# Residuals and layer norms of a two-block kernel: residual added by VectorE from PSUM, squares summed on 32-column tiles, another order of the tail

## The chip, the cores and the metric

One core of one Trainium2 chip runs the whole program. The metric is device time in microseconds (us), the median of several runs; the profile is one further execution, taken by the hardware profiler. Engines: PE is TensorE (PEld its weight loads), DVE is VectorE, ACT is ScalarE, POOL is GpSimd, SP is SyncE. A trailing q (DVEq) is an engine's sequencer.

## The reference, cut to what matters

All is float32. The first block (two layers, 512 latent tokens and 256 context tokens of 1024 channels) feeds a second block; the change touches the end of each mixing part and each feed-forward part of the first block:

```python
x = layer_norm(ALPHA * x + ml[2] * (m @ w_out + b_out), ln1_g, ln1_b)
h = modulate(x, ml[3], ml[4])                  # h * (1 + scale) + shift
x = layer_norm(ALPHA * x + ml[5] * ((silu(dwconv(h @ w_up_a)) * (h @ w_up_u)) @ w_down), ln2_g, ln2_b)
# layer_norm: mean and variance over the 1024 channels of each token, eps 1e-5
```

ALPHA is the square root of 2. Layer 0 does this for latent and context tokens (width W = 768), each stream with its own modulation; layer 1 for the latent tokens alone (W = 512).

## The kernel before

Activations lie channel-major: X is 8 chunks of 128 channels by TOK = 768 tokens. A linear layer is run in units: a unit makes 128 output channels of all W tokens in one PSUM tile. To keep float32 precision, weights and activations are each split in a high and a low part (fp32r), and a unit is three thirds of matmuls, high x high, low weights x high, high weights x low (`unit`, L516). There are four PSUM tiles of 1024 columns; units alternate between two of them (tb and tb + 1), and a semaphore `tile_free` for each tile is raised by whoever empties it. The first two units of a linear layer whose input has just been made run as a pair (`first_pair`, L484), chunk by chunk as high and low parts come in (semaphores h2_hi, h2_lo, ...).

Weights stream through a ring of four slots: SP loads a unit into w_raw, ACT rounds it to w_hi (L1089, `refill`, after the unit that used the slot), and POOL subtracts for w_lo (L447). Each engine runs one instruction list written out in order; semaphores with counted values (`on`, `at_least`) tie them together. The table STAGES only counts how often each stage takes each PSUM tile.

The stages around the change, for each of the two layers: `out` (8 units, tb 0) and norm `ln1`; then `up0`, `down0`, `up1`, `down1`, `up2`, `down2` (the feed-forward channels in parts of 8, 8 and 6 chunks; a unit of down2 has 6 chunks instead of 8; tb 2 for all down stages) and norm `ln2`. After ln1 the modulated input of up0 is made (`modulated`, `modulated_hi`), after ln2 of layer 0 that of layer 1, after ln2 of layer 1 the kernel writes x for the second block. So there are four norm sites: ln1 and ln2, in layer 0 and in layer 1.

How a site works before the change. When unit j is done, ACT moves it from PSUM to SBUF, scaled by the gate (`scaled_residual_unit`, L1172), then refills the weight slot; DVE adds it to X with the factor alpha (L1777 at a norm, L1764 in down0 and down1). The norm's statistics are made while the last units run: a sum over the first four chunks gives a pivot, which PE makes by a matmul with a matrix of ones behind unit 4 (`channel_sum`, L523), and DVE subtracts twice that from each chunk (`pivoted`, L1782); ACT squares each chunk (`layer_norm_square`, L1130) into four buffers, and PE sums squares 0 to 3 behind unit 5, 4 and 5 behind unit 6, and 6, the second half of the mean, and 7 behind unit 7, each with ones of 128x128. Then ACT makes the squared mean and the negated mean (L1136, L1137), DVE the variance (`variance`, L1817), ACT the inverse root as Ln and Exp (L1139, L1141), and DVE adds the negated mean to all chunks (`recentered`, L1809: six before it waits for the root, the last two inside the loop that follows). DVE and ACT then make the modulated input two chunks at a time (L1747, ACT L1116, L1754). At ln2 of layer 0, DVE scales X (L1721) before it raises the last two counts of h_lo (in code behind L1958) that PE waits for; at ln2 of layer 1, DVE scales and shifts each chunk (L1721, L2127).

## Time and profile before

| | |
|---|---|
| median of 3 runs | 3555.5 us (3552.7 to 3559.64) |
| the profiled execution's own time | 3559.22 us |
| its span, first to last instruction | 3557.4 us |
| mean granted TensorE clock over the span | 0.964 of full speed |
| busy: PE / PEld / DVE / ACT / POOL | 93% / 73% / 55% / 35% / 24% |

The busy shares are averages over many stages with different limits. What a site is worth is read from its own stretch: the time from the end of unit 5 to the end of unit 7, and from there to where the next units run unhindered.

### The profile page before, as it was taken

To read this page: it belongs to the slowest core of one execution; us is meant where nothing else is said; L and a number is where in the kernel's file an instruction comes from. 1 tells how busy PE (TensorE), PEld (TensorE's weight loads), DVE (VectorE), ACT (ScalarE), POOL (GpSimd) and SP (SyncE) were. 2 spreads that over 40 slices of the span, in tenths; PEclk is the share of its full clock that TensorE was granted. 3 is DMA by queue.
4 is the path that set the end of the run, shared out by engine and by line. 5 is a ranking of instruction groups with operands and counts; after the bars stand their busy time and mean duration, and the time that the engine had idled before them with its cause. 6 is when DMAs were issued, how large, how long until landed. Compare 5 with 4: busy or idle time off the path is not lost.

```text
span 3557.4 us, 44002 instructions
## 1 busy us (share of the span) xinstructions
PE 3306.4 (93%) x15976; PEld 2583.6 (73%) x15976; DVE 1971.0 (55%) x2633; ACT 1244.2 (35%) x1742; POOL 847.6 (24%) x336
## 2 busy tenths in 40 slices
PE   6999899998889999978999998899997999999997
PEld 4778677787778888856776777588875775677665
DVE  4678987624375252547789854565464534253333
ACT  2112253233233222233225334442235344443533
POOL 1002102222222232320020233244442221332211
PEclk9999899999999999989999999999998989998999
DMA  6541101112111211114510123132231120221111
GB/s 259 172 166 48 36 1 48 48 48 94 43 48 54 71 62 63 60 65 166 198 60 13 60 65 113 54 101 95 95 98 54 53 65 26 75 83 54 54 37 58
DMA packets 72957, 272.08 MB, mean 76 GB/s; under 512 B 8545, under 2 KB 9057, under 8 KB 71905
## 3 DMA queue, kind: packets, MB, share of 16 engines
q1 hardware_dynamic: 71360, 256.04, 21.7%
q10 hardware_dynamic: 1440, 13.89, 1.0%
q8 instruction: 107, 1.75, 0.2%
q14 instruction: 50, 0.40, 0.0%
HBM read 264.66 MB, written 5.24 MB: 76 GB/s over the span
## 4 chain that ended last, share of the span: by engine, by line
PE 81%; DVE 9%; ACT 3%; DVEq 2%; issue 2%; DMA 1%; ACTq 1%; SPq 0%
PE ps L516 47%; PE ps L758 11%; PE ps L484 4%; PE ps L523 3%; PE ps L586 2%; PE ps L707 2%; DVE x L1903 2%; DVE arena L1895 2%; PE ps L894 1%; PE ps L574 1%; PE ps L871 1%; PE ps L607 1%; PE ps L729 1%; PE ps L992 1%; PE ps L973 1%
## 5 line engine op out<-in xcount | busy, mean ns | idle before, releaser
L447 POOL TENSOR_TENSOR w_lo<-w_raw,w_hi 128x1024 fp32r<-128x1024 f32 x332 | 847.4, 2555 | 2670.5 <-ACT w_hi L1089 2670.3
L516 PE MATMUL ps<-act_hi,w_hi 128*128 128x512 f32 x2656 | 565.0, 362 | 7.8 <-DVE arena L2064 2.0
L516 PE MATMUL ps<-act_lo,w_hi 128*128 128x512 f32 x2656 | 545.9, 355 | 0.0
L516 PE MATMUL ps<-act_hi,w_lo 128*128 128x512 f32 x2656 | 545.8, 355 | 0.0
L516 PEld LDWEIGHTS ps<-act_hi,w_hi 128*128 128x128 f32 x2656 | 436.9, 189 | 126.3 <-issue 50.8
L1089 ACT ACTIVATE w_hi<-w_raw 128x1024 fp32r<-128x1024 f32 x380 | 399.8, 1054 | 316.9 <-PE ps L516 91.0
L516 PEld LDWEIGHTS ps<-act_hi,w_lo 128*128 128x128 f32 x2656 | 436.3, 188 | 74.0
L516 PEld LDWEIGHTS ps<-act_lo,w_hi 128*128 128x128 f32 x2656 | 436.3, 188 | 73.5
L1903 DVE SCALAR_TENSOR_TENSOR x<-arena,vec,x 128x512 f32<-128x512 f32 x336 | 234.9, 727 | 0.2 <-issue 0.2
L1895 DVE SCALAR_TENSOR_TENSOR arena<-arena,vec 128x783 f32<-128x783 f32 (+1 forms) x240 | 230.2, 959 | 0.0
L2096 DVE SCALAR_TENSOR_TENSOR arena<-arena,vec 128x769 f32<-128x769 f32 (+1 forms) x88 | 159.1, 1808 | 15.3 <-issue 15.3
L1154 ACT ACTIVATE arena<-ps,vec 128x768 f32<-128x768 f32 (+3 forms) x64 | 50.9, 795 | 293.5 <-PE ps L516 197.0
L758 PE MATMUL ps<-act_hi,w_hi 128*128 128x512 f32 x432 | 138.5, 459 | 12.0 <-ACT vec L1124 6.2
L1764 DVE SCALAR_TENSOR_TENSOR x<-x,arena 128x768 f32 (+1 forms) x32 | 32.5, 1016 | 185.7 <-ACT arena L1172 185.7
L1172 ACT ACTIVATE arena<-ps,mod 128x512 f32<-128x512 f32 x72 | 41.7, 614 | 240.7 <-PE ps L516 182.7
L758 PEld LDWEIGHTS ps<-act_hi,w_hi 128*128 128x128 f32 x432 | 88.2, 210 | 47.3 <-issue 29.6
L1686 DVE TENSOR_TENSOR ffn_lo<-arena,ffn_hi 128x768 f32 (+1 forms) x44 | 118.2, 2687 | 7.1 <-issue 1.3
L1777 DVE SCALAR_TENSOR_TENSOR x<-x,arena 128x768 f32<-128x768 f32 (+1 forms) x32 | 34.6, 1082 | 153.5 <-ACT arena L1172 153.5
L707 PE MATMUL ps<-arena 128*128 128x256 f32 (+1 forms) x288 | 103.8, 481 | 15.8 <-ACT tmp L1197 15.8
L758 PE MATMUL ps<-act_lo,w_hi 128*128 128x512 f32 x432 | 111.5, 391 | 5.6 <-DVE act_lo L2161 5.6
L758 PE MATMUL ps<-act_hi,w_lo 128*128 128x512 f32 x432 | 114.8, 400 | 0.0
L1378 ACT ACTIVATE arena<-ps 128x512 f32<-128x512 f32 x66 | 32.4, 526 | 211.2 <-PE ps L516 208.3
(311 smaller groups left out, 4794.7 us busy)
## 6 DMA issues: line engine op xcount, KB each, us to landing
w_raw<-in_weights SPq DMA_DIRECT2D x380, 512.0 KB, 3.5
arena<-in_ada_w SPq DMA_DIRECT2D x75, 512.0 KB, 4.4
tmp<-in_ada_w SPq DMA_DIRECT2D x21, 512.0 KB, 5.1
x<-in_x SPq DMA_DIRECT2D x2, 1536.0 KB, 20.2
x<-in_x ACTq DMA_DIRECT2D x1, 3072.0 KB, 10.1
x_mid<-x ACTq DMA_DIRECT2D x1, 3072.0 KB, 9.7
x<-x_mid ACTq DMA_DIRECT2D x1, 3072.0 KB, 10.2
arena<-in_pool_w ACTq DMA_DIRECT2D x2, 1024.0 KB, 4.8
```

The costliest lines, as they stand in the source:

```text
L447: nc.gpsimd.tensor_tensor(WL[:, w], raw, WH[:, w].bitcast(f32), ALU.subtract).then_inc(units_split, 1)
L484: last = nc.tensor.matmul(ps(tb + s, a, b), w[:, s * UNIT + k * P:s * UNIT + (k + 1) * P], act[:, k * TOK + a:k * TOK + b], start=(n == 0 ...
L516: last = nc.tensor.matmul(ps(t, a, b), w[:, s * UNIT + k * P:s * UNIT + (k + 1) * P], act[:, k * TOK + a:k * TOK + b], start=(n == 0 and k ...
L523: last = nc.tensor.matmul(ps(s, a, b), ONES[:, :], src[:, a:b], start=start, stop=stop)
L586: last = nc.tensor.matmul(ps(3, (m % 2) * 512, (m % 2) * 512 + 2 * P), values(m, k), AR[:, a:a + 2 * P], start=(k == 0), stop=(k == nk - 1))
L707: last = nc.tensor.matmul(ps(it % 2, a, b), AR[:, q:q + P], AR[:, k + a:k + b], start=True, stop=True)
L758: return nc.tensor.matmul(out, w0[:, k0:k0 + P], act[:, k * n:k * n + SEQ], start=start, stop=stop)
L1089: nc.scalar.activation(WH[:, s * UNIT:(s + 1) * UNIT], RAW[:, (s % 2) * UNIT:(s % 2 + 1) * UNIT], ACT.Copy).then_inc(hi_done, 1)
L1686: return V.tensor_tensor(lo, src, hi.bitcast(f32), ALU.subtract)
L1895: t = V.scalar_tensor_tensor(acc, src, w, acc, ALU.mult, ALU.add)
L1903: t = V.scalar_tensor_tensor(acc, src, w, acc, ALU.mult, ALU.add)
L2096: t = V.scalar_tensor_tensor(cv, src, w, cv, ALU.mult, ALU.add)
```

## The change

1. The residual is added by DVE straight from PSUM: one scalar_tensor_tensor for each token stream, PSUM times gate plus X (`residual`). ACT no longer copies these units out; in out, down0, down1 and down2 it only refills weight slots. The factor alpha and the gated bias of ln1's residual are put on X beforehand (a tensor_scalar for each chunk and stream, while `out` begins); the factor for ln2 is folded into the scale and bias with which ACT writes ln1's output.
2. Squares 0 to 6 are summed by matmuls with a 128x32 matrix (first column ones, the others zeros), each chunk into its own 32 rows of the pivot's PSUM tile: 0 to 3 behind unit 6, 4 to 6 inside unit 7, ahead of its last third, followed by the first part of the second mean. ACT copies the result to SBUF, and behind unit 7 one `channel_sum` adds it, one adds chunk 7 to the mean, and one adds square 7.
3. ACT asks for the table set natural_log_exp_and_others as the stage `out` or `down2` begins.
4. The pivot is subtracted from chunks 5 to 7 before their residual is added. The negated mean is made before the squared mean. DVE recenters chunk 0 before the variance, 1 and 2 between variance and root, and 3 to 7 inside the loop that follows.

```diff
+            def unit(s, t, sp_, kt, hi, lo, within=None):
                 for n, (w, act) in enumerate(((WH, hi), (WL, hi), (WH, lo))):
+                    if within and n == 2:
+                        within()
...
+                def squares(cs):
+                    pe.wait_ge(*at_least(l, nm + "_sq", cs[-1] + 1))
+                    for a, b in sp_:
+                        for c in cs:
+                            j, src = 32 * (c % 4), LN_SQ[c % 4]
+                            last = nc.tensor.matmul(PS[j:j + 32, pivot * 1024 + a:pivot * 1024 + b], FIRST[:, :], AR[:, src + a:src + b],
+                                                    start=(c < 4), stop=(c > 2))
+                    last.then_inc(on(l, nm + "_sq_used"), len(cs))
+                def within():
+                    squares((4, 5, 6))
+                    pe.wait_ge(tile_free[tb], taken(l, nm, tb, 0))
+                    pe.wait_ge(*at_least(l, nm + "_summed", 2))
+                    channel_sum(tb, AR[:, SUM:SUM + TOK], sp_, True, False)
...
-                    for c in {5: (0, 1, 2, 3), 6: (4, 5), 7: (6,)}.get(j, ()):
-                        squares(c)
...
+                    if j == 6:
+                        pe.wait_ge(tile_free[pivot], taken(l, nm, pivot, 1))
+                        squares((0, 1, 2, 3))
                     if j == 7:
+                        pe.wait_ge(tile_free[sq], taken(l, nm, sq, 0))
+                        pe.wait_ge(*at_least(l, nm + "_part", 1))
+                        channel_sum(sq, AR[:, LN_SQ[0]:LN_SQ[0] + TOK], sp_, True, False)
                         pe.wait_ge(*at_least(l, nm + "_centered", CH))
                         channel_sum(tb, X[:, (CH - 1) * TOK:CH * TOK], sp_, False, True).then_inc(on(l, nm + "_mean"), 1)
-                        squares(7)
+                        pe.wait_ge(*at_least(l, nm + "_sq", CH))
+                        channel_sum(sq, AR[:, LN_SQ[3]:LN_SQ[3] + TOK], sp_, False, True).then_inc(on(l, nm + "_sq_used"), 1)
...
+            def refilled_norm(l, nm, st, tb):
+                W, pivot = width(l), 2 - tb
+                nc.scalar.preload_act_table_set("natural_log_exp_and_others")
+                for j in range(CH):
+                    act.wait_ge(units_used, unit_done(l, st, j // SLOTS, j % SLOTS))
+                    refill(l, st, j // SLOTS, j % SLOTS)
+                    for c in {4: (0, 1, 2, 3), 6: (4, 5, 6), 7: (7,)}.get(j, ()):
+                        layer_norm_square(l, nm, c, W)
+                    if j == 6:
+                        act.wait_ge(*at_least(l, nm + "_sq_used", 7))
+                        nc.scalar.activation(AR[:, LN_SQ[0]:LN_SQ[0] + W], ps(pivot, 0, W), ACT.Copy).then_inc(on(l, nm + "_part"), 1)
+                        act.drain().then_inc(tile_free[pivot], 1)
...
+            def residual(l, st, gate, tb, j):
+                t = tb + j % 2
+                dve.wait_ge(units_used, unit_done(l, st, j // SLOTS, j % SLOTS))
+                for m, (a, b) in enumerate(spans(l)):
+                    x = X[:, j * TOK + a:j * TOK + b]
+                    last = V.scalar_tensor_tensor(x, ps(t, a, b), at(MOD, mod(l, gate, j, m), 1), x, ALU.mult, ALU.add)
+                return last
...
+                residual(l, st, gate, tb, 4).then_inc(tile_free[tb], 1)
+                dve.drain()
                 dve.wait_ge(*at_least(l, nm + "_mean", 1))
                 for c in range(5):
+                    pivoted(c).then_inc(on(l, nm + "_centered"), 1)
+                for c in (5, 6, 7):
                     pivoted(c)
+                dve.drain().then_inc(tile_free[pivot], 1)
                 for j in (5, 6):
-                    residual(j)
-                    pivoted(j)
-                    dve.drain()
+                    residual(l, st, gate, tb, j).then_inc(on(l, nm + "_centered"), 1)
+                    dve.drain().then_inc(tile_free[tb + j % 2], 1)
                     V.tensor_tensor(sums, x_(4) if j == 5 else sums, x_(j), ALU.add)
...
+                recentered(l, nm, tb, 0)
                 variance(l, nm, tb, dst)
-                for c in range(6):
+                for c in (1, 2):
                     recentered(l, nm, tb, c)
-                dve.wait_ge(*at_least(l, nm + "_root", 3))
+                dve.wait_ge(*at_least(l, nm + "_root", 4))
+            def recentered_pair(l, nm, tb, i):
+                for c in {1: (3,), 2: (4, 5), 3: (6, 7)}.get(i, ()):
+                    recentered(l, nm, tb, c)
...
+                for c in range(CH):
+                    for m, (a, b) in enumerate(spans(l)):
+                        x = X[:, c * TOK + a:c * TOK + b]
+                        V.tensor_scalar(x, x, ALPHA, at(GB, (l * CH + c) * 2 + m, 1), ALU.mult, ALU.add)
...
                         scale_chunk(l, "ln2", "ln2_g", c, W)
-                        if c < 2:
-                            recentered(l, "ln2", 2, c + 6)
+                        if c + 3 < CH:
+                            recentered(l, "ln2", 2, c + 3)
```

## Rows read from the trace of the kernel before

**Rows 1.** The page, part 4: the chain that ended last, by engine.
```profile
PE 81%; DVE 9%; ACT 3%; DVEq 2%; issue 2%; DMA 1%; ACTq 1%; SPq 0%
```

**Rows 2.** Windows of PE: stretch us, length, busy (instructions), granted clock, DMA share, GB/s.
```profile
941.06:975.72 34.66, 28.36 (x120) 0.90 0.11 31
975.72:996.08 20.36, 7.12 (x17) 0.76 0.08 26
1547.22:1577.25 30.03, 24.09 (x96) 0.89 0.06 18
2249.96:2274.92 24.96, 20.00 (x60) 0.86 0.17 61
2651.24:2670.06 18.82, 14.04 (x48) 1.00 0.25 84
1635.00:1645.00 10.00, 10.00 (x45) 1.00 0.63 211
```

**Rows 3.** The chain in order of time, 888 to 1016 us: start, us, what.
```profile
931.22 1.29 PE ps L523 x4
...
967.18 8.48 PE ps L516 x48
```

**Rows 4.** Timeline of PE, 940 to 1016 us: start, us, operation [idle before <-releaser].
```profile
944.19 7.09 PE L523 MATMUL ps<-arena,ones 128*128 128x512 f32 x16 [3.20 <-ACT arena L1130]
...
1011.35 0.97 PE L484 MATMUL ps<-act_hi,w_hi 128*128 128x512 f32 x4 [0.33 <-ACT act_hi L1116]
```

**Rows 5.** Timeline of ACT, 890 to 1016 us.
```profile
904.18 1.23 ACT L1172 ACTIVATE arena<-ps,gate_bias,mod 128x512 f32<-128x512 f32 x2 [13.99 <-issue]
...
985.33 0.81 ACT L1137 ACTIVATE arena<-ps 128x768 f32<-128x768 f32 x1
...
988.43 1.28 ACT L1141 ACT_TABLE_LOAD   x1
...
1015.47 0.87 ACT L1378 ACTIVATE arena<-ps 128x512 f32<-128x512 f32 x2 [1.81 <-PE ps L484]
```

**Rows 6.** Timeline of DVE, 900 to 1015 us.
```profile
905.52 0.96 DVE L1777 SCALAR_TENSOR_TENSOR x<-x,arena 128x768 f32<-128x768 f32 x1 [8.69 <-ACT arena L1172]
...
978.11 0.96 DVE L1782 SCALAR_TENSOR_TENSOR x<-ps,x 128x768 f32<-128x768 f32 x1
...
987.16 6.17 DVE L1809 TENSOR_TENSOR x<-x,arena 128x768 f32<-128x768 f32 x7 [0.21 <-issue]
993.43 2.20 DVE L1747 SCALAR_TENSOR_TENSOR tmp<-x,ln_mod_gain,arena 128x512 f32<-128x512 f32 x4
```

**Rows 7.** Timeline of POOL, 895 to 1020 us.
```profile
978.15 2.35 POOL L447 TENSOR_TENSOR w_lo<-w_raw,w_hi 128x1024 fp32r<-128x1024 f32 x1 [13.69 <-ACT w_hi L1089]
```

**Rows 8.** Timeline of DVE, 2255 to 2370 us (layer 1).
```profile
2265.80 2.42 DVE L1797 TENSOR_TENSOR arena<-arena,x 128x512 f32<-128x512 f32 x1
...
2286.42 1.42 DVE L1747 SCALAR_TENSOR_TENSOR tmp<-x,ln_mod_gain,arena 128x512 f32<-128x512 f32 x2
```

**Rows 9.** Timeline of PE, 1530 to 1660 us.
```profile
1622.82 1.22 PE L484 MATMUL ps<-act_lo,w_hi 128*128 128x512 f32 x2 [4.29 <-DVEq L1958]
...
1633.24 1.07 PE L607 MATMUL ps<-arena,gla_w 128*32 128x512 f32 x8
1634.24 2.12 PE L516 MATMUL ps<-act_hi,w_hi 128*128 128x512 f32 x8
```

**Rows 10.** Timeline of DVE, 2615 to 2735 us.
```profile
2678.76 3.70 DVE L1809 TENSOR_TENSOR x<-x,arena 128x512 f32<-128x512 f32 x6 [0.21 <-issue]
2682.56 0.75 DVE L1721 SCALAR_TENSOR_TENSOR x<-x,vec,arena 128x512 f32<-128x512 f32 x1
```

**Rows 11.** Timeline of ACT, layer 1: 2301 us, then 2713 us.
```profile
2301.82 0.60 ACT L1378 ACTIVATE arena<-ps 128x512 f32<-128x512 f32 x1 [1.13 <-PE ps L484]
...
2713.30 1.28 ACT L1124 ACT_TABLE_LOAD   x1
```

**Rows 12.** Timeline of DVE, 60 to 110 us: two-operand tensor_scalar, 512 and 256 columns.
```profile
69.45 0.75 DVE L1901 TENSOR_SCALAR x<-arena,vec 128x512 f32<-128x512 f32 x2
```

More of the change, by code:

```diff
@@ L165, in two_blocks @@
         MASK = sb("gla_masks", 2 * P, i32)
-        ARENA_N = 20318
+        ARENA_N = 20280
         with nc.sbuf_tensor("arena", [P, ARENA_N], f32) as AR:
@@ L470, in single @@
                     start(i, s)
-                    unit(s, tb + s % 2, sp_, kt, hi, lo).then_inc(units_used, 1)
+                    unit(s, tb + s % 2, sp_, kt, hi, lo, within if within and i * SLOTS + s == CH - 1 else None).then_inc(units_used, 1)
                     if behind:
@@ L748, in block1 @@
                     linear(l, f"down{p}", 2, sp_, n, GH, GL, ready=(("g_split", first), ("g_split", first)), tb=2,
-                           behind=layer_norm(l, "ln2", sp_, 2) if p == 2 else None)
+                           **(layer_norm(l, "ln2", sp_, 2) if p == 2 else {}))
             one = ((0, SEQ),)
@@ L1164, in evacuate @@
                         evacuate_unit(l, st, i, s, dst(i, s, W), func, bias)
-            def scaled_residual_unit(l, st, gate, bias, dst, done, first, tb, i, s):
-                act.wait_ge(units_used, unit_done(l, st, i, s))
-                act.wait_ge(*at_least(l, done, i * SLOTS + (first + s + 1)))
-                act.sem_inc(paced[0], 1)
-                for j, (a, b) in enumerate(spans(l)):
-                    last = nc.scalar.activation(AR[:, dst + s * TOK + a:dst + s * TOK + b], ps(tb + s % 2, a, b), ACT.Identity,
-                                                bias=at(GB, i * 8 + (l * CH * 2 + 2 * s + j), 1) if bias else 0.0,
-                                                scale=at(MOD, i * 8 + mod(l, gate, s, j), 1))
-                last.then_inc(tile_free[tb + s % 2], 1)
-                refill(l, st, i, s)
@@ L1178, in scaled_residual, with refilled @@
-            def scaled_residual(l, st, gate, bias, dst, done, first, tb, nm=None):
-                if nm:
-                    for j in range(CH):
-                        scaled_residual_unit(l, st, gate, bias, dst, done, first, tb, j // SLOTS, j % SLOTS)
-                        for c in {5: (0, 1, 2, 3), 6: (4, 5), 7: (6, 7)}.get(j, ()):
-                            layer_norm_square(l, nm, c, width(l))
-                else:
-                    with act.Fori(0, 2) as i:
-                        for s in range(SLOTS):
-                            scaled_residual_unit(l, st, gate, bias, dst, done, first, tb, i, s)
+            def refilled(l, st):
+                with act.Fori(0, 2) as i:
+                    for s in range(SLOTS):
+                        act.wait_ge(units_used, unit_done(l, st, i, s))
+                        refill(l, st, i, s)
@@ L1386, in block1 @@
                     if p == 0:
-                        layer_norm_out(l, "ln1", "ln1_b", W)
-                    scaled_residual(l, f"down{p}", 5, False, FT, "res2", p * CH, 2, "ln2" if p == 2 else None)
+                        layer_norm_out(l, "ln1", "ln1_b", W, ALPHA)
+                    if p < 2:
+                        refilled(l, f"down{p}")
+                    else:
+                        refilled_norm(l, "ln2", "down2", 2)
                 layer_norm_root(l, "ln2", 2, LN_R, W)
@@ L1757, in modulated, with add_residual, layer_norm_input @@
                         last.then_inc(on(l, nm + "_lo"), 1)
-            def add_residual(l, st, src, done, alpha):
-                with dve.Fori(0, 2) as i:
-                    for s in range(SLOTS):
-                        dve.wait_ge(tile_free[2 + s % 2], emptied(l, st, 2 + s % 2, use(i, s)))
-                        x = at(X, (i * SLOTS + s) * TOK, width(l))
-                        V.scalar_tensor_tensor(x, x, alpha, AR[:, src + s * TOK:src + s * TOK + width(l)], ALU.mult, ALU.add)\
-                            .then_inc(done, 1)
-            def layer_norm_input(l, nm, st, src, done, alpha, tb):
+            def residual(l, st, gate, tb, j):
[5 more added lines that the diff above has]
+                return last
+            def add_residual(l, st):
+                for j in range(CH):
+                    residual(l, st, 5, 2, j).then_inc(tile_free[2 + j % 2], 1)
+            def layer_norm_input(l, nm, st, gate, tb):
                 W, pivot = width(l), 2 - tb
@@ L2112, in block1 @@
                     if p < 2:
-                        add_residual(l, f"down{p}", FT, on(l, "res2"), ALPHA if p == 0 else 1.0)
-                layer_norm_input(l, "ln2", "down2", FT, on(l, "res2"), 1.0, 2)
+                        add_residual(l, f"down{p}")
+                layer_norm_input(l, "ln2", "down2", 5, 2)
                 normalized(l, "ln2", 2, LN_R)
                 if l == 0:
-                    modulated(1, "h", BOTH, lambda i: recentered(l, "ln2", 2, i + 6) if i < 2 else None)
+                    modulated(1, "h", BOTH, lambda i: recentered_pair(l, "ln2", 2, i))
                     scale(l, "ln2", "ln2_g", W)
```

77 lines of the change are left out of this document (33 added, 44 removed).

## The prediction

> **What bounds the kernel now.** The page's chain that ended last comes first: PE holds 81% of it, DVE 9%, ACT 3% [rows 1], so time is won only where PE waits or does work that can go. The waits of PE, longest first, then point to the norm sites, and windows put between the ends of PE's units show what each site costs. From the end of unit 5 to the end of unit 7, four sites take 34.66, 30.03, 24.96 and 18.82 us [rows 2]. A unit of layer 0 takes 8.48 us [rows 3]; scaled by its chunks (6 of 8 in down2) and tokens (512 of 768) two units are 16.96, 12.72, 11.30 and 8.48. The remainder, 17.70, 17.31, 13.66 and 10.34 us, is sums of squares and waits for them. Once after each of units 5, 6 and 7, PE waits some 3 us for ACT's square, then runs the sums; the granted clock of the first stretch is 0.90, in undisturbed units 1.00 [rows 2, 4]. The second part of each site is the tail behind unit 7: from 975.72 PE has 7.12 us of work in 20.36 us [rows 2], until DVE's modulated input starts at 993.43 [rows 6].
>
> **Part one, to the end of unit 7.** Removed: three waits a site and seven of eight full sums of squares. Put in: a group of four 32-column matmul streams behind unit 6, a group of three in unit 7, and one mean sum. The kernel already has such a group: the four 128x32 streams of 512 columns at 1633.24 give way to the next unit after 1.00 us [rows 9], against 1.29 us for one full sum of 768 columns, so 0.86 for 512 [rows 3]. A group is 1.0 us for 512 columns and, by proportion, 1.5 for 768. Layer 0 then has 1.5 + 1.5 + 1.29 = 4.3 us above its two units, layer 1 has 1.0 + 1.0 + 0.86 = 2.9. Gains: 13.4, 13.0, 10.8 and 7.4, together 44.6 us. Bounds of a group: 0.86 from below, and from above its streams one after another, 7 x 1.29 = 9.0 instead of 3.0 in layer 0 and 6.0 instead of 2.0 in layer 1, 20 us over four sites. I take the row, which has the same form.
>
> For this no new wait may arise. Squares 0 to 3 are made after unit 4, two units (8.5 us at least) before use. Squares 4 to 6 can start when the first group has released the buffers, 1.0 to 1.5 us after unit 6, and take 3 x 0.84 us at most (an ACT operation of this width is 0.81 [rows 5]); PE comes to them after two thirds of unit 7, 2.8 us later in the shortest site, against some 1.6 for the three squares of 512 columns. ACT's copy of the part sums has the last third of unit 7 and the mean sum before it, 1.4 + 0.86 us for 0.6. Tight, but covered; without cover it costs at most 1 us a site.
>
> The Trainium skill, "TensorEngine Tiling (Array Packing)", Key Properties, says that a change of tiling mode drains TensorE, which speaks against mixing groups with full units. The trace bounds this: with both changes inside, the group of four is 1.00 us, 0.14 above one sum of 512 columns [rows 3, 9]; by row and rule together the sum stays as it is.
>
> **Part two, the tail, layer 0.** Let 0 be the end of unit 7.
> - DVE's residual: 512 and 256 columns from PSUM. The nearest row, a 768-column operation with PSUM and X, is 0.96 [rows 6]; ACT's two pieces are 1.23 [rows 5]. I take 1.05 and start 0.1: done 1.15.
> - PE: part sum 0 to 1.29, chunk 7 of the mean to 2.6, square 7 to 3.9 (ACT: refill to 1.15, square to 2.0).
> - ACT's copy, 0.81 [rows 5], to 3.45. DVE recenters chunk 0 (6.17/7 = 0.88 [rows 6]) behind POOL's weight pass, which now runs from 1.35 to 3.7 (2.35 [rows 7]): done 4.6. Variance 0.96, to 5.55.
> - ACT: Ln and Exp without the two loads of 1.28 us [rows 5], about 0.98 + 0.84 and hand-overs: 7.5. Chunks 1 and 2 fit beneath. The modulated input starts at 7.75; before it was 993.43 - 975.72 = 17.71 [rows 2, 6]. Gain 9.96.
> - Given back: the loop now holds five recenterings instead of one, 4 x 0.88 = 3.5. DVE and ACT feed that pair of units (PE waits for ACT's high part at 1011.35 [rows 4]; the pair is done at 1015.4 [rows 5]), so it counts in full. Gain 6.4.
> - ln2 of layer 0 has the same steps; there PE's last two chunks wait for DVE until 1622.82, after it has also scaled X [rows 9]. All of DVE's work moves along: 6.3.
>
> **The tail, layer 1.** Residual done 0.8, part sum 0.86, mean 1.7, copy 2.35. But a tensor_tensor of two SBUF inputs that meets POOL's pass takes 2.42 us instead of 0.62 (3.70/6) [rows 8, 10], so chunk 0 is done at 4.3, not 3.1; the scalar_tensor_tensor at 978.11, with one input in PSUM, ran at 0.96 though POOL started at 978.15 [rows 6, 7]. Variance 5.0, root 6.45, next step 6.6. At ln1 it was 2286.42 - 2274.92 = 11.50 [rows 2, 8]: gain 4.9, less 4 x 0.62 = 2.5 inside the loop, 2.4. The pair ends at 2301.8 [rows 11], 15.4 after that step; with 2.5 more it is feed-bound at 17.9. At ln2 it was 2682.56 - 2670.06 = 12.50 [rows 2, 10]: 5.9, less 3 x 0.62 (five instead of two recenterings): 4.0. The set with both functions is still loaded when the second block takes its first root, so the load of 1.28 us between Ln and Exp at 2713.30, on PE's path, goes too [rows 11]: 5.3. Tails: 6.4 + 6.3 + 2.4 + 5.3 = 20.4 us.
>
> The Trainium skill, "SBUF — State Buffer", SBUF: two separate sides, says that a VectorE operation with two SBUF inputs and a GpSimd operation exclude each other for a whole instruction; the rows show that (2.42 against 0.62), and it holds nothing against the new residual, which has one SBUF input. Without any blocking, layer 1's two tails would be 1.1 us shorter each.
>
> **Costed at nothing.** The 16 tensor_scalars that put alpha and bias on X: two take 0.75 us [rows 12], so 6.0 in layer 0. DVE is idle for 8.69 us to 905.52 and the pair ends near 904.1 [rows 5, 6], so 7.3 us hide them; at the 0.96 us of a slower form, 0.4 would show, and with no cover all 6. PSUM emptied by DVE: after each of eight pairs PE waits for the first emptying, 1.23 us with ACT [rows 5] and 1.15 with DVE; elsewhere a whole unit covers it. Bounds 1 us either way over all pairs. ACT's 64 copies that vanish were off the path, as is the early load. SP gains no DMA; weight refills start up to 1.2 us earlier, and POOL with them.
>
> **Sum.** 44.6 + 20.4 = 65.0. From the profiled execution's 3559.2 us this gives 3494; that run lies 3.7 above the median, so against the median 3490.5. I predict 3491. The tail steps are good to 1.5 us a site, the 256-column groups to 2 in all, the pairs to 1: 3481 to 3500 for this case.
>
> **Rivals.**
> - *Forecast*, 0.61.
> - *The groups do not overlap*, 0.10: 20 us back, 3511. Against it stands the group of four at 1.00 us. For it: those streams read data that DMA brought, not squares, but nothing there bears on the array.
> - *The tail gives nothing*, 0.11: the recentering moved into the pair, fed in bursts at a low clock (the tail's stretch has 0.76 [rows 2]), eats it: 44.6 alone, 3511. Against it: the loads and two square sums leave a chain that nothing else covers.
> - *The table loads stay*, 0.08: if each function keeps its own load, 4 x 2.57 + 1.28 = 11.6 back, 3502.
> - *DVE empties PSUM too late*, 0.05: if POOL blocks the residual as it does tensor_tensor, it takes 2.4 us instead of 0.96, 64 times; if all 64 showed (64 x 1.45 = 93), it would be 3584. But PE needs the tile a unit later, 4.2 us at least, so only the eight first ones of pairs can show, before POOL starts: no more than 12 us, 3503.
> - *The clock*, 0.03, ends slower. If the 32-column groups count as little work and PE stays at 1.2 GHz from unit 6 to the end of the pair, two units cost 49 us more over four sites, groups and sums 14, and the pairs 17 beyond their feed (8.5, 3.4, 4.7): 80 against the 65 won, so 3555.5 + 15 = 3571. It decides from four fifths of that stretch on. Against it: behind the group at 1633.24 the clock is 1.00 [rows 2, 9].
> - *Little or nothing changes*, 0.02: these sites are not on the path. The chain runs through them, so hardly.
>
> **Range.** 3476 to 3513: it takes in the serial groups, the lost tails and the staying loads, and below it leaves 5 us for waits that I have not counted. What a measurement of this kernel can tell from no change is 0.2%, 7 us: faster 0.93, the same 0.03, slower 0.04.
>
> **What the profile after would show.** In layer 0, 21 us from the end of unit 5 to that of unit 7 at ln1 (34.66 now), 17 at ln2; in layer 1, 14.2 and 11.4. No wait of PE for ACT's squares; four 128x32 streams in 1.0 us; no table load between Ln and Exp; the modulated input 7.75 us after unit 7 in layer 0, 6.6 in layer 1; more pauses in PE's pair, whose feed is now the longer chain. Wrong would be: a stretch near 25 us (groups serial), a granted clock under 0.9 in unit 7, DVE residuals over 2 us, or PE waiting for DVE in the middle of down stages.

## The result, and the profile after

| | before | after |
|---|---|---|
| median in the first measurement (4 runs each) | 3554.8 us (3552.7 to 3559.64) | 3491.18 us (3486.87 to 3496.76) |
| the profiled execution's own time, its span | 3559.22, 3557.4 us | 3492.35, 3490.6 us |
| mean granted clock over the span | 0.964 | 0.966 |

The ratio is 0.982, 95% interval 0.9802 to 0.9838: 64 us faster; 3491 was predicted. A second measurement of the changed kernel, beside three experiments, gave 3489.23 us and 0.9806 (0.9793 to 0.982).

The page's header, busy shares and chain of the changed kernel, against [rows 1]:

```profile
span 3490.6 us, 43799 instructions
...
PE 3280.6 (94%) x15988; PEld 2563.1 (73%) x15988; DVE 1965.0 (56%) x2693; ACT 1179.1 (34%) x1636; POOL 846.5 (24%) x336
...
PE 82%; DVE 9%; ACT 3%; DVEq 2%; issue 2%; DMA 1%; ACTq 1%; SPq 0%
```

The shares of the chain hardly move, as they must when 64 of 3555 us go. The windows do, cut at the same places as [rows 2]: end of unit 5 to end of unit 7 at the four sites, and behind the first one the stretch until PE's next matmul.

```profile
942.01:963.40 21.39, 21.39 (x131) 16.34 (x130) 4.20 (x6) 5.25 (x6) 6.22 (x2) 1.00 0.15 50
963.40:973.64 10.24, 4.13 (x13) 1.92 (x12) 7.10 (x11) 6.45 (x9) 2.36 (x1) 0.86 0.17 51
1524.46:1541.70 17.24, 17.24 (x107) 12.64 (x106) 6.65 (x8) 5.24 (x6) 5.51 (x2) 1.00 0.10 31
2207.11:2221.40 14.29, 14.29 (x66) 9.64 (x65) 2.89 (x4) 4.28 (x6) 4.86 (x2) 1.00 0.27 97
2594.08:2605.83 11.75, 11.75 (x54) 7.41 (x53) 5.64 (x6) 4.28 (x6) 5.04 (x3) 1.00 0.43 134
```

PE (second and third number) is busy for the whole of each stretch, at a granted clock of 1.00; it was 0.86 to 0.90 in three of them. PE's timeline at the first site shows what fills it:

```profile
947.56 2.94 PE L519 MATMUL ps<-act_lo,w_hi 128*128 128x512 f32 x16
950.42 1.50 PE L545 MATMUL ps<-arena,ones_in_first_column 128*32 128x512 f32 x16
951.85 3.09 PE L519 MATMUL ps<-act_hi,w_hi 128*128 128x512 f32 x16
954.78 2.99 PE L519 MATMUL ps<-act_hi,w_lo 128*128 128x512 f32 x16
957.70 1.49 PE L545 MATMUL ps<-arena,ones_in_first_column 128*32 128x512 f32 x12
959.12 1.56 PE L526 MATMUL ps<-arena,ones 128*128 128x512 f32 x4
960.33 3.13 PE L519 MATMUL ps<-act_lo,w_hi 128*128 128x512 f32 x16
...
973.64 1.62 PE L485 MATMUL ps<-act_hi,w_hi 128*128 128x512 f32 x4 [6.11 <-ACT act_hi L1130]
...
985.80 0.96 PE L485 MATMUL ps<-act_hi,w_hi 128*128 128x512 f32 x4 [1.69 <-ACT act_hi L1130]
...
992.35 0.96 PE L485 MATMUL ps<-act_hi,w_hi 128*128 128x512 f32 x4 [2.12 <-ACT act_hi L1130]
...
997.55 3.02 PE L519 MATMUL ps<-act_hi,w_hi 128*128 128x512 f32 x16 [0.71 <-ACT arena L1388]
```

Before, the same stretch held two waits of some 3 us (one is in [rows 4]) and six full sums, and the third wait stood right behind unit 7:

```profile
962.71 4.48 PE L523 MATMUL ps<-arena,ones 128*128 128x512 f32 x8 [3.11 <-ACT arena L1130]
...
978.76 4.54 PE L523 MATMUL ps<-arena,ones 128*128 128x512 f32 x8 [3.11 <-ACT arena L1130]
```

Now no row of the stretch carries a wait. The group of four gives way to the next unit after 951.85 - 950.42 = 1.43 us, the group of three after 1.42: both within 0.1 of the 1.5 predicted. The price stands further down: in the pair PE now pauses twice for ACT's high part.

DVE and ACT in the same tail:

```profile
963.49 1.14 DVE L1778 SCALAR_TENSOR_TENSOR x<-ps,mod,x 128x512 f32<-128x512 f32 x2 [10.72 <-PE ps L519]
967.12 0.96 DVE L1824 TENSOR_TENSOR x<-x,arena 128x768 f32<-128x768 f32 x1 [2.49 <-ACT arena L1150]
968.00 0.95 DVE L1832 SCALAR_TENSOR_TENSOR arena<-ps,arena 128x768 f32<-128x768 f32 x1
969.09 1.83 DVE L1824 TENSOR_TENSOR x<-x,arena 128x768 f32<-128x768 f32 x2
970.99 2.21 DVE L1760 SCALAR_TENSOR_TENSOR tmp<-x,ln_mod_gain,arena 128x512 f32<-128x512 f32 x4
```

```profile
968.98 0.94 ACT L1154 ACTIVATE arena<-arena,cst 128x768 f32<-128x768 f32 x1 [1.19 <-DVE arena L1832]
969.99 0.84 ACT L1156 ACTIVATE arena<-arena 128x768 f32<-128x768 f32 x1
```

The residual takes 1.14 us, not 2; Ln and Exp follow each other without a load; the modulated input starts 970.99 - 963.40 = 7.6 us behind unit 7, where it was 17.7 [rows 2, 6].

I divide each site at three marks: end of unit 5, end of unit 7, start of the variance, and the start of the next unit that is not part of a pair (at the last site: PE's first work behind the second block's root). Gain of each part, before less after, from the two timelines:

| site | units 6 and 7 (predicted) | unit 7 to variance | variance to next unit | both tail parts (predicted) |
|---|---|---|---|---|
| ln1, layer 0 | 34.66 - 21.39 = 13.3 (13.4) | 10.3 - 4.6 = 5.7 | 30.5 - 29.6 = 0.9 | 6.6 (6.4) |
| ln2, layer 0 | 30.03 - 17.24 = 12.8 (13.0) | 10.1 - 4.6 = 5.5 | 39.7 - 38.7 = 1.0 | 6.5 (6.3) |
| ln1, layer 1 | 24.96 - 14.29 = 10.7 (10.8) | 6.2 - 4.3 = 1.9 | 21.5 - 20.5 = 1.0 | 2.8 (2.4) |
| ln2, layer 1 | 18.82 - 11.75 = 7.1 (7.4) | 7.8 - 4.3 = 3.5 | 38.2 - 37.0 = 1.3 | 4.8 (5.3) |
| sum, before rounding | 43.8 (44.6) | 16.5 | 4.2 | 20.8 (20.4) |

43.8 + 20.8 = 64.6 of the spans' 66.8 us; the rest is the balance of the stretches up to and between the sites, where 4.4 us were won, and of the second block, where 2.2 us were lost. From the first site's variance to the last one's, two profiles of the changed kernel differ by 4.3 us (1642.1 and 1646.4), so neither of the two says much by itself. The column to look at is the fourth: at the sites, all of the new order and the table set is worth 4.2 us. Its single entries are good to 1.5 us only. In the second profile of the changed kernel (experiment 9) the first and the last site take 31.1 and 35.7 us instead of 29.6 and 37.0, because TensorE's clock comes back at another matmul of the pair, and the sum over the four sites is 4.0.

### The profile page after: what moved, and what is told of

The parts are those of the page before. It is cut to its first block, busy times and chain, and to the rows that moved or that the text cites. A ratio compares the mean times of both kernels' runs of the same rounds, so it can differ in the third digit from the quotient of the medians.

```text
span 3490.6 us, 43799 instructions
## 1 busy us (share of the span) xinstructions
PE 3280.6 (94%) x15988; PEld 2563.1 (73%) x15988; DVE 1965.0 (56%) x2693; ACT 1179.1 (34%) x1636; POOL 846.5 (24%) x336
## 4 chain that ended last, share of the span: by engine, by line
PE 82%; DVE 9%; ACT 3%; DVEq 2%; issue 2%; DMA 1%; ACTq 1%; SPq 0%
PE ps L519 47%; PE ps L772 11%; PE ps L485 4%; PE ps L600 2%; PE ps L721 2%; PE ps L526 2%; DVE arena L1916 2%; DVE x L1924 2%; PE ps L908 1%; PE ps L588 1%; PE ps L885 1%; PE ps L621 1%; PE ps L743 1%; PE ps L1006 1%; PE ps L987 1%
## 5 line engine op out<-in xcount | busy, mean ns | idle before, releaser
L1778 DVE SCALAR_TENSOR_TENSOR x<-ps,mod,x 128x512 f32<-128x512 f32 x96 | 60.2, 658 | 288.2 <-PE ps L519 238.1
L600 PE MATMUL ps<-arena 128*128 128x256 f32 x416 | 103.6, 382 | 1.7 <-ACT arena L1321 1.5
L2118 DVE TENSOR_SCALAR arena<-arena,vec 128x769 f32<-128x769 f32 (+1 forms) x44 | 29.1, 661 | 132.1 <-ACT arena L1388 132.1
## 6 DMA issues: line engine op xcount, KB each, us to landing
x<-in_x ACTq DMA_DIRECT2D x1, 3072.0 KB, 10.1
```

The lines of the kernel that those rows point to most:

```text
L600: last = nc.tensor.matmul(ps(3, (m % 2) * 512, (m % 2) * 512 + 2 * P), values(m, k), AR[:, a:a + 2 * P], start=(k == 0), stop=(k == nk - 1))
```

## Experiments

Every time stands beside the kernel before on the same chip (3559.38, 3558.35 and 3557.18 us in three batches). The last mark before the second block is the start of the variance of the last site; in the changed kernel it was 2610.1 us in one profiled execution and 2612.2 in the other.

**1. The 32-column tiles.** The same order, but squares 0 to 6 by full 128x128 matmuls.

```diff
-                            j, src = 32 * (c % 4), LN_SQ[c % 4]
-                            last = nc.tensor.matmul(PS[j:j + 32, ...], FIRST[:, :], AR[:, src + a:src + b], start=(c < 4), stop=(c > 2))
+                            last = nc.tensor.matmul(ps(pivot, a, b), FIRST[:, :], AR[:, src + a:src + b], start=(c == 0), stop=(c == 6))
```

> The changed kernel, but squares 0 to 6 are summed by full 128x128 matmuls (first column ones), one after another in the same PSUM rows; waits, positions and the number of copies stay. Theory one (the four 32-column streams overlap): the seven squares cost 7 x 1.29 = 9.0 us in layer 0 and 6.0 in layer 1 instead of some 3.0 and 2.0, so 20 us more than the changed kernel's 3491, 3511, and 27 us instead of 21.4 from the end of unit 5 to that of unit 7 at layer 0's ln1. Rival (the gain was the waits alone, a group costs what full sums cost): 3491.

Measured: 3515.75 us, ratio 0.9879 (0.9865 to 0.9894). Its PE timeline at the first site, then at the last:

```profile
950.04 5.32 PE L545 MATMUL ps<-arena,ones_in_first_column 128*128 128x512 f32 x16
955.01 3.13 PE L519 MATMUL ps<-act_hi,w_hi 128*128 128x512 f32 x16
...
960.75 4.03 PE L545 MATMUL ps<-arena,ones_in_first_column 128*128 128x512 f32 x12
...
2619.78 3.60 PE L545 MATMUL ps<-arena,ones_in_first_column 128*128 128x512 f32 x8
...
2626.01 2.74 PE L545 MATMUL ps<-arena,ones_in_first_column 128*128 128x512 f32 x6
```

The changed kernel has 1.50 and 1.49, 1.07 and 1.06 us there. The length of a row includes some overlap with the next one; from the end of unit 5 to the end of unit 7 the four sites are 5.7, 5.9, 3.6 and 3.6 us longer than in the changed kernel, 18.8 in all for the 20 worked out. The ratio differs by 0.0059 from that of the first measurement, which is 21 us. The four streams do run side by side: full sums give way to the next unit after 955.01 - 950.04 = 4.97 us, the group of four after 1.43, and the group of three after 1.42.

**2. Squares made and summed one unit later.** ACT squares chunks 0 to 3 behind unit 5, PE sums them there.

```diff
-                    for c in {4: (0, 1, 2, 3), 6: (4, 5, 6), 7: (7,)}.get(j, ()):
+                    for c in {5: (0, 1, 2, 3), 6: (4, 5, 6), 7: (7,)}.get(j, ()):
...
-                    if j == 6:
+                    if j == 5:
                         pe.wait_ge(tile_free[pivot], taken(l, nm, pivot, 1))
                         squares((0, 1, 2, 3))
```

> The changed kernel, but ACT makes squares 0 to 3 only after unit 5 and PE sums them right behind unit 5, as in the order of the kernel before; 32-column groups stay. Theory one (the wait came from ACT's place for the squares): PE waits 1.06 + 4 x 0.84 + 0.2 = 4.6 us behind unit 5 in layer 0, 3.3 in layer 1, 16 us over four sites, and up to 6 more for the lower clock after the wait: 3507 to 3513. Rival (the groups are cheap enough, PE has other slack): 3491.

Measured: 3517.42 us, 0.9883 (0.9868 to 0.9898). PE at the first site:

```profile
945.46 2.05 PE L545 MATMUL ps<-arena,ones_in_first_column 128*32 128x512 f32 x16 [4.34 <-ACT arena L1144]
947.44 4.06 PE L519 MATMUL ps<-act_hi,w_hi 128*128 128x512 f32 x16
```

The wait is back, 4.34 us, and with it what hangs on it: the group takes 2.05 instead of 1.50 us and the next third of a unit 4.06 instead of 3.09, at a granted clock of 0.71 from 945.4 to 951.3 us. One wait a site costs 5.9, 5.7, 5.0 and 5.3 us at the four sites, 21.9 in all; by ratio and by median the total is 22 and 26 us longer, above the 3507 to 3513 us expected. Each taken back by itself, the place of the sums (21.9 us) is worth about as much as the 32-column tiles (18.8). Together that is 40.7 of the 43.8 us of this part; the kernel before had two such waits in the stretch, and how the rest divides no run shows.

**3. Without the request for one table set.**

```diff
-                nc.scalar.preload_act_table_set("natural_log_exp_and_others")
```

> The changed kernel without the request for the common table set. Theory one: the root is now the chain that ends last at each norm, so both loads show at four sites, 4 x 2.57, and one of 1.28 at the second block's first root: 11.6 more, 3503. Rival (the loads lie beneath DVE's recentering or come early anyway): 3491.

Measured: 3501.03 us, 0.984 (0.9827 to 0.9853). ACT in its first tail:

```profile
965.32 1.28 ACT L1154 ACT_TABLE_LOAD   x1
966.62 0.94 ACT L1154 ACTIVATE arena<-arena,cst 128x768 f32<-128x768 f32 x1
967.61 1.28 ACT L1156 ACT_TABLE_LOAD   x1
968.90 0.84 ACT L1156 ACTIVATE arena<-arena 128x768 f32<-128x768 f32 x1
```

The first load, 965.32 to 966.60, runs beneath DVE's variance (965.43 to 966.38), so that a norm shows one load, not two: DVE goes on with the modulated input 4.4, 4.4 and 3.5 us behind the variance instead of 3.0, 3.0 and 2.2, and at the last site with its first product after 3.5 instead of 2.2. That is 5.4 us over four norms.

But the total is 10 us longer (12 by ratio against the second measurement), and the rest is in the second block. The request for the set acts there too: without it ACT has ten more table loads behind the last variance, up to 156 us from it. The last of the two loads for the second block's root shows 1.3 us: PE waits 2.19 us for what follows it, in place of 0.90, and then needs 1.6 us more for its next sixteen matmuls. Four loads stand before the next norm of the second block. PE there, without the request and then in the changed kernel (experiment 9):

```profile
2767.78 3.66 PE L772 MATMUL ps<-act_hi,w_hi 128*128 128x512 f32 x8 [3.08 <-ACT vec L1138]
```

```profile
2758.46 2.06 PE L772 MATMUL ps<-act_hi,w_hi 128*128 128x512 f32 x8 [0.38 <-ACT vec L1138]
```

The wait is 2.7 us longer, and the eight matmuls behind it take 1.6 us more. From the 600th to the 800th matmul behind the last variance the two kernels without the request (this one and the kernel before) take 35.2 and 35.0 us, every other one 30.7 to 31.6. So the request is worth 5.4 + 1.3 + 1.6 + 4.3 = 12.6 us in the changed kernel. The span of this profile is 12.7 us longer than the control's, but other stretches of the two scatter by some us as well. The expectation's 11.6 (3503 us) nearly came out, but with other terms: it had both loads at every norm, and nothing of these four or of the slower matmuls.

**4. The request alone, in the kernel before.**

```diff
                 if nm:
+                    nc.scalar.preload_act_table_set("natural_log_exp_and_others")
                     for j in range(CH):
```

> The kernel before with one addition, the request for the common table set at the head of out and down2. Theory one: there DVE's seven recenterings (6.2 us in layer 0, 3.7 to 4.3 in layer 1) run longer than Ln and Exp with both loads (4.5), so the loads were hidden; only the second block's first root gains 1.3: 3553.5. Rival (the loads stand on the path in the kernel before as well): 11.6 less, 3543.

Measured: 3567.53 us over ten runs, ratio 1.0025 (1.0015 to 1.0034): slower, and both expectations missed. DVE in its first tail, to be held beside [rows 6]:

```profile
987.66 6.17 DVE L1810 TENSOR_TENSOR x<-x,arena 128x768 f32<-128x768 f32 x7 [0.21 <-issue]
993.93 2.21 DVE L1748 SCALAR_TENSOR_TENSOR tmp<-x,ln_mod_gain,arena 128x512 f32<-128x512 f32 x4
```

ACT's root is done at 989.33 here and was at 990.57 before; DVE recenters seven chunks until 993.8 either way. In the kernel before the loads lay wholly beneath that. From variance to next unit nothing was won at three sites (31.1, 39.7, 21.2 against 30.5, 39.7, 21.5), and 1.3 at the last, the load of the second block's root. In the second block the four loads are gone as well, and the 800th matmul behind the last variance starts 4.3 us earlier (178.2 against 182.5 us behind it). All of that is lost again behind this point, and 10 us more; where stands under 9.

**5. The old order of recentering, with all the rest.**

```diff
-                for c in (1, 2):
+                for c in (1, 2, 3, 4, 5):
                     recentered(l, nm, tb, c)
...
-                for c in {1: (3,), 2: (4, 5), 3: (6, 7)}.get(i, ()):
+                for c in {0: (6,), 1: (7,)}.get(i, ()):
```

> The changed kernel with the old places of the recentering: chunk 0, variance, chunks 1 to 5, then 6 and 7 inside the loop. Theory one (DVE feeds the pair, so its work counts wherever it stands): the modulated input starts some 3 us later in layer 0 and the loop is 3 us shorter; 1 to 2 us more in all, 3493. Rival (the early start counts, the loop hides its recentering): 3.5 + 3.5 + 2.5 + 1.7 = 11 us more, 3502.

Measured: 3491.5 us, 0.9812 (0.9799 to 0.9825), no difference. From variance to next unit: 29.6, 38.7, 20.7 and 35.5 us, against 29.6, 38.7, 20.5 and 37.0 in the first profile of the changed kernel and 31.1, 38.7, 20.5 and 35.7 in the second. At the first site PE starts 3.5 us later and then hardly pauses (0.33 us in place of 1.69 and 2.12). At the last site DVE's act_lo (L2186) stands behind all its recenterings, 16.7 us behind the variance in either order; with the new order PE starts 1.8 us earlier (5.6 instead of 7.4 us behind the variance) and waits for it 1.7 us longer. PE there in the changed kernel, first and second profile, then in this one:

```profile
2626.80 1.22 PE L772 MATMUL ps<-act_lo,w_hi 128*128 128x512 f32 x2 [7.32 <-DVE act_lo L2186]
```

```profile
2628.92 1.22 PE L772 MATMUL ps<-act_lo,w_hi 128*128 128x512 f32 x2 [7.33 <-DVE act_lo L2186]
```

```profile
2628.40 1.22 PE L772 MATMUL ps<-act_lo,w_hi 128*128 128x512 f32 x2 [5.58 <-DVE act_lo L2186]
```

So the 1.5 us between 37.0 and 35.5 do not belong to the order: with the same wait the second profile has 35.7. They are the clock behind the wait, which over the next 5 us is 0.50 in the first profile, 0.67 in the second and 0.71 here.

**6. The pass over X twice** (the second one multiplies by 1).

```diff
+                for c in range(CH):
+                    for m, (a, b) in enumerate(spans(l)):
+                        x = X[:, c * TOK + a:c * TOK + b]
+                        V.tensor_scalar(x, x, 1.0, CST[:, 2:3], ALU.mult, ALU.mult)
```

> The changed kernel with a second pass over X behind the pass of alpha and bias, times 1 (16 more tensor_scalars in layer 0, 8 in layer 1; the values stay). Theory one (the first pass is hidden in DVE's idle time with about 1.7 us to spare in layer 0): the second, 5.4 us, shows by 3.7 there, and by under 1 in layer 1: 3495. Rivals: wholly hidden, 3491; both passes on the path already, 9 us more, 3500.

Measured: 3502.93 us, the median of three executions (a fourth took 9303.68 us, for a reason that nothing here shows, and is left out); the ratio with its interval is 0.9854 (0.9835 to 0.9872). PE's first unit behind the pair of `out`, in the changed kernel, then here:

```profile
906.88 3.07 PE L519 MATMUL ps<-act_hi,w_hi 128*128 128x512 f32 x16 [0.98 <-DVE x L1778]
```

```profile
908.93 4.60 PE L519 MATMUL ps<-act_hi,w_hi 128*128 128x512 f32 x16 [3.13 <-DVE x L1778]
```

With one pass DVE is done 1.70 us before PE's pair; the second, 5.36 us, sticks out by 2.15 and leaves the next third of a unit 1.5 us longer. So the single pass is covered, and one twice as long costs 3.7 us of layer 0. The other 8 us of the median are not at this place (9).

**7. Every residual of down0 and down1 twice**, in two separate measurements.

```diff
                 for j in range(CH):
+                    dve.wait_ge(units_used, unit_done(l, st, j // SLOTS, j % SLOTS))
+                    dve.drain()
+                    for m, (a, b) in enumerate(spans(l)):
+                        V.scalar_tensor_tensor(AR[:, GT + a:GT + b], ps(2 + j % 2, a, b), ..., ALU.mult, ALU.add)
                     residual(l, st, 5, 2, j).then_inc(tile_free[2 + j % 2], 1)
```

> The changed kernel, but in down0 and down1 DVE computes each residual twice, the first time into unused space; PSUM is released after the second. Theory one (only the first tile of a pair is waited for): 2 x 1.14 in layer 0 and 2 x 0.66 in layer 1: 3.6 us more, 3495. Rival (DVE's emptying stands on the path unit by unit): 16 x 1.14 + 16 x 0.66 = 29 us more, 3520.

> Every residual of the two parts down0 and down1 computed a second time by VectorE, as measured already. Leaves nothing out. Theory: the 12 us that it is behind the changed kernel belong to the program (its granted clock behind the last layer norm of the first block falls at other places), and come again: 3500 to 3506 us. Rival: they were of that batch; 3490 to 3495 us.

Measured: 3503.47 us, 0.985 (0.9837 to 0.9863), and 3505.92 us, 0.9852 (0.9836 to 0.9867). The waits of PE for the residual, grouped, in the changed kernel and in the first of these:

```profile
PE ps L519 <- DVE x L1778: 6.9, 8, 1.1
```

```profile
PE ps L519 <- DVE x L1778: 10.6, 8, 2.2
```

The columns are us in total, times, longest. Only eight emptyings show, one behind each pair, and doubling 32 of the 64 adds 3.7 us. The variance of the last site is at 2612.4 and 2617.5. The rest of the 12 to 17 us is again elsewhere.

**8. X scaled once**, my try at a better kernel, in two measurements: X is multiplied by the root once, ACT makes the modulated value twice from it, and the scaling products in the feed-forward part go.

```diff
-                            last = V.scalar_tensor_tensor(TMP[...], at(X, ...), at(LNG, ...), AR[:, r + a:r + b], ALU.mult, ALU.mult)
+                            V.tensor_tensor(x, x, AR[:, r:r + W], ALU.mult).then_inc(on(l, nm + "_t"), 1)
...
+                            last = nc.scalar.activation(dst, X[:, c * TOK + a:c * TOK + b], ACT.Identity,
+                                                        bias=at(LNB, 2 * c + j, 1), scale=at(LNG, 2 * c + j, 1))
```

> A version meant to be faster. X is multiplied by the inverse root once, in place; ACT makes the modulated value twice from X (gain and bias as scale and bias), as float32 and as rounded high part, DVE subtracts; DVE's products for chunks 2i and 2i+1 stand ahead of the low parts of the two chunks before. ln's gain goes into ACT's scale, so DVE's scaling passes (7.5 us behind the loop at layer 0's ln2) go. Theory one (DVE feeds the pair of units): its loop falls from 23 to 21 x 0.88 = 18.5 us at two sites, 7.5 go at ln2 of layer 0, 1 to 2 at layer 1's ln1: 18 us less, 3473. Rival (ACT, now 4.4 us for two chunks, becomes the feed's limit and the hand-overs eat the rest): only the 7.5 show, 3483. Second rival: DVE's scaling was covered by PE's pair: 3491.

> X multiplied by the root once in place, both modulated parts from it, the eight scaling products gone; as measured already, nothing left out. Beside the changed kernel on the same chip. Theory: it is ahead by 4 to 8 us at equal clock and comes out in two groups again, 3475 to 3480 us where the mean clock is 0.967 or more, 3490 to 3498 us at 0.962 or 0.963; median 3478 to 3495 us. Rival: no two groups; always 3490 us or more, which would make it no better than the changed kernel.

Measured: 3492.75 us, 0.9798 (0.9776 to 0.982), and 3495.52 us, 0.9827 (0.9813 to 0.984), beside which the changed kernel ran at 0.9806. It reaches the last variance at 2603.5 and 2603.8 us, 6 to 9 us ahead, and loses all of it behind that mark. The two groups of the expectation did not come again: all five executions of the second measurement took 3494.33 to 3498.26 us. It beats nothing.

**9. The control, and a delay at the last site.**

> The changed kernel itself once more, beside the kernel before and the two that follow. Theory: the two kernels that had come out 8 to 15 us behind their working (the residual added twice, X scaled once) lost it in the records' granted clock, whose mean was 0.960 to 0.962 in all five executions of the first and 0.962 or 0.963 in three of the second, against 0.965 to 0.969 here; so this kernel comes out at a ratio of 0.980 to 0.983 again, 3486 to 3498 us, with a clock of at least 0.965. Rival: the chip of that batch ran everything slower, which the kernel before, 3558.35 us there and 3554.8 us in the first measurement, speaks against; then this one is at 3500 us or more too.

```diff
                 W, sq = width(l), 3 - tb
+                if l == 1 and nm == "ln2":
+                    dve.drain()
+                    for k in range(2):
+                        V.memset(AR[:, CV:CV + 1544], 0.0)
+                        dve.drain()
```

> Two fills of 1,544 numbers per partition (some 2.8 us by the 0.74 us of an 814-number fill) put ahead of the variance of the last layer norm of layer 1 alone, and nothing else changed; nothing left out. Nothing covers them: the pair of the second block's root starts later by them. If time behind the last layer norm is a fixed sum of work, this is 2.8 us slower than the changed kernel beside it (3493 to 3497 us). Theory: the moment at which the second block begins shifts the stretches of lower granted clock behind it (0.67 to 0.92 at 100 to 140 us and 520 to 600 us behind the norm, different from kernel to kernel), so that the difference is anything from -8 to +14 us, and goes with the mean clock in the records at some 3 us for each 0.001.

Measured: 3489.23 us for the changed kernel, 3490.13 us, 0.9812 (0.9799 to 0.9826), with the delay. The fills put 3.8 us between PE's last sum and the variance (5.1 against 1.3), yet the total is 0.9 us longer. A fixed sum of work would give 3.8, but the executions of either kernel scatter by 8 and 12 us, so this alone settles nothing.

The profiles say more. Behind the last variance every kernel here runs the same 3468 matmuls, and DVE the same 593 operations. ACT has 542 or 543 instructions there in the kernels with the request, and 554 or 555 in the two without it. Windows from 100 to 280 us behind that mark, of the kernel before, the control, experiment 4, the first of 7 and the second of 8:

```profile
2777.80:2957.80 180.00, 168.16 (x761) 124.77 (x760) 76.17 (x132) 79.47 (x111) 43.02 (x18) 0.90 0.16 53
```

```profile
2712.20:2892.20 180.00, 171.99 (x760) 124.92 (x758) 76.94 (x141) 77.17 (x115) 40.53 (x17) 0.90 0.17 53
```

```profile
2778.40:2958.40 180.00, 171.21 (x722) 124.37 (x718) 70.24 (x122) 69.47 (x97) 41.70 (x18) 0.82 0.17 53
```

```profile
2712.40:2892.40 180.00, 171.11 (x713) 124.36 (x712) 69.66 (x122) 69.54 (x98) 41.17 (x18) 0.82 0.17 53
```

```profile
2703.80:2883.80 180.00, 171.12 (x713) 123.96 (x711) 69.26 (x122) 70.08 (x99) 40.77 (x18) 0.82 0.17 53
```

PE is as busy in all of them, but gets through 760 matmuls at a granted clock of 0.90 and 713 to 722 at 0.82. From the last variance to the end of the span:

| kernel | clock in the window | to the end, us | mean clock of its timed executions |
|---|---|---|---|
| control; 5; before | 0.90 | 874.2; 875.5; 879.6 | 0.965 to 0.969; 0.964 to 0.966; 0.960 to 0.966 |
| after, first profile; 3; 6 | 0.86 to 0.87 | 880.5; 885.8; 883.7 | 0.965 to 0.969; 0.963 to 0.966; 0.963 to 0.964 |
| delay; 1; 2 | 0.85 | 880.6; 880.6; 881.1 | 0.965 to 0.968; 0.964 to 0.967; 0.961 to 0.965 |
| 7, both | 0.82, 0.84 | 889.2, 886.4 | 0.960 to 0.962, 0.960 to 0.965 |
| 8, both | 0.81, 0.82 | 892.1, 888.7 | 0.962 to 0.968, 0.962 to 0.964 |
| 4 | 0.82 | 889.7 | 0.956 to 0.962 |

So the 8 to 20 us by which 4, 7 and 8 miss their working are for the most part lost behind the last place that they change, to a lower granted clock. One profile cannot place a kernel: the two of the changed kernel are 6.3 us apart. The largest difference between them is one step, of which a part comes back later: from the 1000th to the 1200th matmul behind the last variance, the control, the kernel before, 3 and 5 take 64.7 or 64.8 us (control: clock 0.95), and all the others 72.8 (first profile of the changed kernel: 0.86). But in part it is a property of the program, since it comes again: the nine executions of 7 take 3502.4 to 3507.0 us, the nine of the changed kernel 3484.8 to 3496.8. Within 8 it splits the executions: 3475.92 and 3479.0 us at 0.967 and 0.968, 3492.75 to 3497.41 at 0.962 and 0.963. What in a program chooses the one or the other stays open: 4 and the kernel before reach the last variance within 0.6 us of each other, and still have 0.82 and 0.90 (they differ there in the ten table loads).

## Why the prediction was right, and where only its sum was

- **Part one, 44.6 us: 43.8 measured**, each stretch within 0.4 us of its number. What it names as removed, three waits and seven full sums, is one of each too many for this stretch: two waits and six sums lay in it, the third wait and the sum of square 6 behind unit 7. The gains were worked out from what stays, so the sum does not depend on this. That the groups overlap was taken from the four streams at 1633.24 [rows 9]; experiment 1 shows what the other reading would have cost, 18.8 us at the sites for the 20 worked out. *The groups do not overlap* is refuted as a description of the changed kernel, and right as a price.
- **"For this no new wait may arise."** None did. Experiment 2 gives the price of a wait: a site loses 5.9 us to a wait of 4.3, since the clock falls with it (0.71 in the 5.9 us behind it).
- **The Trainium skill, "TensorEngine Tiling (Array Packing)", Key Properties**, says that a change of tiling mode drains TensorE. A group of four with both changes inside is 1.43 us for 768 columns, 0.14 above one full sum [rows 3], as the 0.14 seen at 512 columns. So both drains together cost 0.14 us at most; that TensorE drains at all, no row shows.
- **The tails, 20.4 us: 20.8 measured**, and the modulated input at 7.6 and 6.5 us, for 7.75 and 6.6. But the prediction told the tail as one sum. The profiles divide it: 16.5 us come from what lay between unit 7 and the variance (ACT's copy, two additions, two square sums), 4.2 from everything behind. What each of these steps is worth was not run by itself.
- **"The table loads stay", 11.6 us: 12.6, but not by its terms.** It has two loads at each of four norms. A norm shows one, 5.4 us in all, since the first runs beneath the variance. The load at the root is 1.3, as worked out; the 1.6 us that PE loses behind it and the 4.3 us of four loads further on in the second block are in no sum (experiment 3). That the total comes near is luck.
- **What the sum left out.** These 1.6 and 4.3 us are also missing from the forecast, in which the request has no effect behind the second block's first root. The profile after has both (30.7 instead of 35.0 us for the second). They did not show in the total: behind the root the changed kernel is still 2.2 us slower than the kernel before (843.5 against 841.3 in the two profiles), at a clock of 0.86 against 0.90 in the window of experiment 9. So 65 us forecast and 64 measured agree in part by luck: a gain and a loss that were both not counted offset each other.
- **The set and the order at the norms.** In the kernel before both loads were hidden beneath seven recenterings (experiment 4), in the changed one one is: the new order is what exposes it, and the set repays that. By itself the set gave nothing at three norms (experiment 4), and beside the set the order gives nothing at any (experiment 5). The 0.9 to 1.0 us that remain at three sites fit chunk 0's recentering (0.96, in layer 1 0.68), which moved ahead of the variance, where DVE would wait for ACT. That is argued from the rows and was not run by itself.
- **"Given back", 3.5, 3.5, 2.5 and 1.9: right.** Experiment 5 finds the pair fed by DVE and ACT whatever the order, and at the last site the 1.8 us by which PE starts earlier are gone at act_lo. There 5.3 were predicted, and the two profiles have 4.8 and 6.1, by the clock behind the wait.
- **"Costed at nothing": right, by 1.70 us.** That is DVE's idle time between pass and pair (experiment 6).
- **DVE empties PSUM too late**: the residual took 1.14 us, 0.75 for its 512 columns also where POOL's pass runs all the while (2580.82 us), so nothing blocks it, and eight waits show, as the rival had it (experiment 7).
- **The clock** did not fall at the sites (1.00 in all four stretches). It is the rival's place that was wrong: the clock moved in the second block, where the change only takes ten table loads out, with 874 to 892 us for the same matmuls. The prediction hit its number also because the changed kernel takes 874 and 880 us there and not 886 to 892, as experiments 7 and 8 do.

## What to carry to other kernels

Ask of each hidden load or order what hides it, and price the edits in the order in which they uncover each other: at the first three norms the table set was worth nothing until the recenterings left from above it. Ask of a state that an edit sets, such as the loaded table set, where it ends: here it reached 147 us into the next part. Put sums a whole unit behind the operation that makes their input, so that PE never stops; a stop of 4.3 us cost 5.9 here, since the clock fell to 0.71 behind it. And where a kernel runs PE at over 90%, compare variants by the time to the last changed place as well as by the total: some 10 us of the total here depended on where the clock fell behind it.

## What the runs showed of the hardware that I had not expected

- The granted clock in the second block takes different courses in programs with the same instructions there (those with the request), and in two executions of one program: 0.81 to 0.90 over one 180 us window, 874 to 892 us for the same 3468 matmuls; 0.86 and 0.90, 880.5 and 874.2 us for the changed kernel.
- A request that does no more than take table loads out, in the norms' tails and at ten places of the second block, made the kernel before slower, by 0.25% (0.15 to 0.34%). Its rows show no loss at the sites, and it is 4.3 us ahead in the second block before it falls back; its window behind the last norm the lower clock.
- A table load of 1.28 us that ran beneath DVE's variance cost 0.15 us in layer 0 (1.43 less 1.28 for the other load) and nothing in layer 1; the load behind it showed in full.
- In layer 1 POOL's pass made DVE's recentering of chunk 0 take 1.70 us, not 2.42 as predicted from [rows 8]: POOL's pass (2607.30 to 2609.65) had been running for 1.2 us when it began at 2608.51.
